# Head of a hybrid GLA / SSD layer: conditioning tiles issued without waits, x of block 0 normalised on ScalarE, five conditioning tiles contracted on TensorE, first weight units loaded and split first

## The reference, cut to what matters

```python
c_act = silu(c)
ada = c_act @ ada_w + ada_b                      # 1024 -> 3 x 1024
shift, scale, gate = split(ada, 3)
h = rms_norm(x, pre_norm_w) * (1 + scale) + shift    # x: 2048 x 1024
proj = h @ w_in
...
mixed = concat(gla(proj), ssd(proj)) @ w_out
x = x + gate * rms_norm(mixed, post_norm_w)
```

## Time and profile before

| | |
|---|---|
| median of 3 runs | 1800.64 us (1799.56 to 1802.90) |
| profiled execution | 1801.82 us |
| its span, first to last instruction | 1800.1 us |
| TensorE busy in the span | 1670.9 us (93%) |
| VectorE, ScalarE, POOL busy | 876.5, 784.0, 242.2 us |
| mean granted TensorE clock | 0.971 of full speed |

### The profile page before, as it was taken

How to read it: one execution, slowest core, us unless ns; L and a number is a source line. 1 busy time by engine, 2 the same in 40 slices (tenths; PEclk the granted TensorE clock), 3 DMA queues, 4 the chain that set the end, 5 groups by cost and what they waited for, 6 DMA issues and landing times. The chain is left out here.

```text
span 1800.1 us, 27177 instructions
## 1 busy us (share of the span) xinstructions
PE 1670.9 (93%) x10134; PEld 1431.9 (80%) x10134; DVE 876.5 (49%) x1603; ACT 784.0 (44%) x1390; POOL 242.2 (13%) x369
## 2 busy tenths in 40 slices
PE   3688899998999999989999999999999599999998
PEld 2477788887888888878888887888888377888886
DVE  5344344454434443355776668776777442222221
ACT  4354565444444554454455555455444431111110
POOL 5000000010000000000221222222222100000000
PEclk9799999999999999999999999999999799999999
DMA  9321242234222421224111234122110263222221
GB/s 278 130 89 60 82 148 86 66 117 141 77 65 64 142 65 59 82 59 135 65 66 64 93 102 138 65 72 92 66 52 35 103 235 117 93 93 93 93 99 41
DMA packets 105344, 172.23 MB, mean 96 GB/s; under 512 B 7587, under 2 KB 75443, under 8 KB 102310
## 3 DMA queue, kind: packets, MB, share of 16 engines
q1 hardware_dynamic: 102118, 154.05, 26.5%
q10 hardware_dynamic: 2304, 16.78, 2.5%
q0 software_dynamic: 832, 0.22, 0.3%
HBM read 137.21 MB, written 33.82 MB: 95 GB/s over the span
## 5 line engine op out<-in xcount | busy, mean ns | idle before, releaser
L1026 PE MATMUL ps<-hl,w 128*128 128x512 f32 x1488 | 377.5, 403 | 0.1
L1913 PE MATMUL ps<-d_w,d_yh 128*128 128x512 f32 x1536 | 353.0, 392 | 17.7 <-DVE d_yh L1870 11.0
L1913 PEld LDWEIGHTS ps<-d_w,d_yh 128*128 128x128 f32 x1536 | 289.5, 189 | 81.3 <-DVE d_yh L1870 11.4
L1026 PEld LDWEIGHTS ps<-hl,w 128*128 128x128 f32 x1488 | 276.9, 190 | 58.6 <-issue 1.4
L1646 PE MATMUL ps<-hl,w 128*128 128x256 f32 x2304 | 295.3, 288 | 4.3 <-PEq L258 4.3
L1646 PEld LDWEIGHTS ps<-hl,w 128*128 128x128 f32 x2304 | 283.2, 193 | 12.4 <-issue 12.4
L1032 PE MATMUL ps<-w,hl 128*128 128x256 f32 x1536 | 205.4, 291 | 2.0 <-DVE w L738 2.0
L1032 PEld LDWEIGHTS ps<-w,hl 128*128 128x128 f32 x1536 | 195.4, 195 | 4.9 <-DVE w L738 2.4
L1650 PE MATMUL ps<-hl 128*128 128x512 f32 x768 | 178.6, 391 | 0.0
L1528 DVE SCALAR_TENSOR_TENSOR c_acc<-c_before,conv_col,c_acc 128x256 f32<-128x256 f32 x288 | 142.1, 494 | 65.3 <-ACT c_acc L1412 58.3
L1650 PEld LDWEIGHTS ps<-hl 128*128 128x128 f32 x768 | 143.0, 188 | 29.2
(11 more groups left out here) (227 smaller groups left out, 2190.4 us busy)
## 6 DMA issues: line engine op xcount, KB each, us to landing
x_sb<-h SPq DMA_DIRECT2D x52, 512.0 KB, 3.9
c_ac<-step_sums ACTq DMA_DIRECT2D x16, 1024.0 KB, 4.7
w_raw<-in_w_in SPq DMA_DIRECT2D x30, 512.0 KB, 5.0
c_h_raw<-h SPq DMA_DIRECT2D x56, 256.0 KB, 2.8
d_y_raw<-mixed_in SPq DMA_DIRECT2D x7, 2048.0 KB, 9.1
ada<-in_ada_w SPq DMA_DIRECT2D x16, 512.0 KB, 11.4
x_sb<-in_x SPq DMA_DIRECT2D x16, 512.0 KB, 7.4
mixed_in<-y SPq DMA_DIRECT2D x32, 256.0 KB, 2.5
```

The costliest lines, as they stand in the source:

```text
L1026: mm = pe.matmul(ps[:, PROJ + u % 2, :], w[:, u, k, a, :], hl[:, par, k, b, :], start=(k == 0 and i == 0), stop=(k == KT - 1 and i == 2))
L1913: mm = pe.matmul(ps[:, 2 * t + j, :], yh[:, t, f, a, :], w[:, f, c, j * 512:(j + 1) * 512], start=(f == 0 and i == 0), stop=(f == FT - 1 a ...
```

## The change

The edits are all in `front`, in the part ahead of `step(0)`:

- SP: `load_ada` no longer waits. There are eight semaphores still, one for each pair of r in a half, and each reader waits for both tiles of a pair. x of block 0 is issued behind two conditioning tiles instead of one. w units 0 and 1 leave SP's stream. x of block 1 is issued ahead of w unit 2.
- ScalarE issues w units 0 and 1 as its first instructions, on its own queue. It normalises x of block 0, with four activations, in VectorE's place. `w_high` of units 0 and 1 stands ahead of the eight `first_copy`. `w_high` of unit 2 and the squares of block 1 stand behind the last `high`, ahead of `code_part`.
- VectorE adds up conditioning tiles r = 3 to 7 of half 0 and r = 2 to 7 of half 1 (OWN = (3, 2) is the number that it leaves out). `w_low` of units 0 and 1 stands ahead of `gains(0)`, pairs 0 and 2 stand ahead of the additions of half 1, and `w_low` of unit 2 and `x_normed(1)` ahead of `code_sum(0)`.
- TensorE contracts the tiles that are left out, `mods_row(j, r)`: eight products with a tile as weights and a column of c_act. Those of half 0 stand ahead of the transposes, those of half 1 behind the units of k = 1 and k = 2.

```diff
--- before.py
+++ after.py
@@ -123,6 +123,7 @@
     MODS = (7, 5)
     STEPS = GH * NB
     HK = KT // 2
+    OWN = (3, 2)
     SIZES_AT, GATE_AT = NB + 1, NB + 2
 
     W_SLOTS = tuple(2 * u + 3 for u in range(UV))
@@ -259,10 +260,9 @@
             @block.sync
             def _(sp):
                 def load_ada(j, r):
-                    wait(sp, ada_loaded[r], j * 16)
                     src = ada_w[0, r * P:(r + 1) * P, 0:2 * D].rearrange("p (s n) -> p s n", s=2)
                     sp.dma_start(ada[:, j, r, :].rearrange("p (s n) -> p s n", s=2), src[:, :, j * HK * P:(j + 1) * HK * P]
-                                 ).then_inc(ada_loaded[r], 16)
+                                 ).then_inc(ada_loaded[j * HK + r // 2], 16)
 
                 def load_x(b):
                     wait(sp, turned, b * KT)
@@ -313,14 +313,12 @@
                 sp.dma_start(c_col[:, :], c.rearrange("a (k p) -> p (a k)", p=P), allow_slow_non_contiguous=True).then_inc(c_loaded, 16)
                 for r in range(KT):
                     load_ada(0, r)
-                    if r == 0:
+                    if r == 1:
                         load_x(0)
-                load_w(0, 0)
-                load_w(0, 1)
                 for r in range(KT):
                     load_ada(1, r)
+                load_x(1)
                 load_w(0, 2)
-                load_x(1)
                 for k in range(KT):
                     store_h(0, k)
                 load_w(0, AHEAD)
@@ -632,6 +630,9 @@
                         if m >= NB and i in H_SLOTS:
                             again_high(m, H_SLOTS.index(i))
 
+                for u in range(2):
+                    src = column(0, u)
+                    act.dma_start(w_raw[:, u], w_rows[:, :, src:src + P]).then_inc(raw_loaded[u], 16)
                 act.wait_ge(c_loaded, 16)
                 act.activation(c_act[:, :], c_col[:, :], ACT.Silu).then_inc(c_ready, 1)
                 act.preload_act_table_set("natural_log_exp_and_others")
@@ -643,10 +644,13 @@
                 act.wait_ge(consts_ready, 10)
                 act.activation(w2[0:RANK, :], w2_raw[:, :], ACT.Copy).then_inc(w2_hi, 1)
                 act.activation(w2[R0:R0 + RANK, :], w2_raw[:, :], ACT.Copy).then_inc(w2_hi, 1)
+                act.wait_ge(xrstd_ready, 1)
+                for t in range(TB):
+                    act.activation(x_sb[:, t, :], x_sb[:, t, :], ACT.Copy, scale=x_rstd[:, t:t + 1]).then_inc(xn_ready, 1)
+                w_high(0, 0)
+                w_high(0, 1)
                 for k in range(KT):
                     first_copy(k)
-                w_high(0, 0)
-                w_high(0, 1)
                 for k in range(0, KT, 2):
                     act.wait_ge(gain_ready, k // HK + 1)
                     if k == 0:
@@ -654,15 +658,14 @@
                     even_full(0, k, first_full[:, k, :])
                     high(0, k)
                     high(0, k + 1)
-                    if k == HK - 2:
-                        w_high(0, 2)
+                w_high(0, 2)
+                for t in range(TB):
+                    x_square(1, t)
                 code_part(0)
                 evacuate(0, 0)
                 evacuate(0, 1)
                 code_high(0)
                 w_high(0, 3)
-                for t in range(TB):
-                    x_square(1, t)
                 for n in range(STEPS):
                     step(n)
 
@@ -888,12 +891,12 @@
                                       ALU.mult).then_inc(gate_step, 1)
 
                 def add_ada(j, r):
-                    dve.wait_ge(ada_loaded[r], (j + 1) * 16)
-                    if r == 0:
+                    dve.wait_ge(ada_loaded[j * HK + r // 2], 32)
+                    if r == OWN[j]:
                         dve.tensor_scalar(ada_sum[:, j, :], ada[:, j, r, :], c_act[:, r:r + 1], None, ALU.mult
                                           ).then_inc(sum_ready, 1)
                     else:
-                        dve.wait_ge(sum_ready, j * KT + r)
+                        dve.wait_ge(sum_ready, j * (KT - OWN[0]) + r - OWN[j])
                         dve.scalar_tensor_tensor(out=ada_sum[:, j, :], in0=ada[:, j, r, :], scalar=c_act[:, r:r + 1],
                                                  in1=ada_sum[:, j, :], op0=ALU.mult, op1=ALU.add).then_inc(sum_ready, 1)
 
@@ -912,35 +915,31 @@
                     low(0, k + 1)
 
                 dve.wait_ge(c_ready, 1)
-                for r in range(KT):
+                for r in range(OWN[0], KT):
                     add_ada(0, r)
-                    if r == KT // 2:
-                        x_normed(0)
                 dve.wait_ge(wg_hi, 1)
                 dve.tensor_tensor(wg[:, :, L0:L0 + RC], wg_raw[:, :, :], wg[:, :, 0:RC].bitcast(F32),
                                   ALU.subtract).then_inc(wg_ready, 1)
                 dve.wait_ge(w2_hi, 2)
                 dve.tensor_tensor(w2[L0:L0 + RANK, :], w2_raw[:, :], w2[0:RANK, :].bitcast(F32),
                                   ALU.subtract).then_inc(w2_ready, 1)
+                w_low(0, 0)
+                w_low(0, 1)
                 dve.wait_ge(cols_loaded, 32)
                 gains(0)
                 dve.wait_ge(first_raw, KT)
                 first_pair(0)
-                w_low(0, 0)
-                w_low(0, 1)
-                for r in range(KT):
+                first_pair(2)
+                for r in range(OWN[1], KT):
                     add_ada(1, r)
-                    if r == 1:
-                        first_pair(2)
-                    if r == 3:
-                        w_low(0, 2)
                 gains(1)
                 first_pair(4)
                 first_pair(6)
+                w_low(0, 2)
+                x_normed(1)
                 code_sum(0)
                 code_low(0)
                 w_low(0, 3)
-                x_normed(1)
                 for n in range(STEPS):
                     step(n)
 
@@ -974,10 +973,18 @@
 
             @block.tensor
             def _(pe):
-                def mods(j):
-                    pe.wait_ge(sum_ready, (j + 1) * KT)
+                def mods_row(j, r):
+                    pe.wait_ge(ada_loaded[j * HK + r // 2], 32)
+                    for f in range(KT):
+                        pe.matmul(ps[:, MODS[j], f:f + 1], ada[:, j, r, f * P:(f + 1) * P], c_act[:, r:r + 1], start=False,
+                                  stop=False)
+
+                def mods_start(j):
                     bias = ada_col[:, :].rearrange("p (s k) -> p s k", s=2)[:, :, j * HK:(j + 1) * HK]
                     pe.matmul(ps[:, MODS[j], 0:KT].rearrange("p (s k) -> p s k", s=2), ident[:, :], bias, start=True, stop=False)
+
+                def mods(j):
+                    pe.wait_ge(sum_ready, (j + 1) * KT - sum(OWN[:j + 1]))
                     for f in range(KT):
                         mm = pe.matmul(ps[:, MODS[j], f:f + 1], ada_sum[:, j, f * P:(f + 1) * P], ones[:, 0:1], start=False,
                                        stop=(f == KT - 1))
@@ -1131,14 +1138,22 @@
                             sum_gate()
 
                 pe.wait_ge(consts_ready, 8)
+                pe.wait_ge(c_ready, 1)
+                pe.wait_ge(cols_loaded, 32)
+                mods_start(0)
+                for r in range(OWN[0]):
+                    mods_row(0, r)
                 pe.wait_ge(xn_ready, TB)
                 for k in range(KT):
                     wait(pe, first_raw, k - 3)
                     turn_x(0, k, FIRST_TURNS[k % 4])
-                pe.wait_ge(cols_loaded, 32)
                 mods(0)
+                pe.wait_ge(first_raw, KT)
+                mods_start(1)
                 for k in range(HK):
                     first_units(k)
+                    if 0 < k <= OWN[1]:
+                        mods_row(1, k - 1)
                 mods(1)
                 for k in range(HK, KT):
                     first_units(k)
```

## The result

| | before | changed |
|---|---|---|
| median | 1800.39 us (6 runs, 1799.56 to 1802.90) | 1787.65 us (6 runs, 1784.45 to 1791.43) |
| ratio | | 0.9929, 95% interval 0.9916 to 0.9942 |
| profiled execution, span | 1801.82, 1800.1 us | 1787.65, 1785.9 us |
| first unit, second gains G, T | 36.65, 57.42, 82.36 | 37.25, 52.80, 69.97 |

The kernel is 12.7 us (0.7%) faster by medians and 14.2 by the spans of the two profiled executions. The forecast was 1791.0 in a range of 1786 to 1796.5, on the scale of the median.

What follows compares the result with a forecast made beforehand. TensorE's waits for x and VectorE were taken to bound the head. T comes 9.6 us earlier, 7.3 of it from G to T; 1801.82 less 9.6 gives 1792.2, on the median's scale 1791.0, range 1786 to 1796.5.

Steps and rivals of the forecast that it cites:

- first unit: Start of TensorE's first unit products in the head: forecast at 37.1 us, against 36.65 before.
- second gains G: Time when the gains of the second modulation are ready: forecast 55.2 us, 2.2 us earlier than before.
- T: First transpose of block 1 on TensorE: forecast 72.8 us, 9.6 us earlier; its shift carries to the end.
- Loads: DMA at the start: w adds 2.45 us ahead of x, ada tile 1 2.0; last x tile at 18.3 us.
- The first gains: Gains of the first modulation: forecast 34.4 us, set by VectorE and the loads, 2.2 us later than before.
- the clock charge ahead of G: TensorE before the second gains: one stretch of about 3.4 us at half speed, charged as 1.7 us.
- What bounds G: Before the second gains: VectorE's additions end under TensorE's work; two rows moved to TensorE cost 3.9 us and still pay.
- Behind T: After block 1's first transpose: no gain counted, at most 3.1 us more if the shorter wait keeps TensorE's clock high.
- Only the back half pays: Rival: second gains stay about 57.4 us, only the order behind them gains; 1792 to 1796.5 us, chance 0.26.
- Clock low throughout: Rival: TensorE slow at every step before the second gains, which come at 62.4; 1798 to 1802.5 us, chance 0.07.
- mutual slowing of the queues: Rival: three DMA queues slow each other from the start, tile 7 near 55 us, kernel about 1817 us; chance 0.05.
- The change does not do what it says: Rival: early w or fewer additions would bring nothing alone; no own chance, covered by the back-half case's time.

Runs made afterwards that it cites:

- the kernel with w on SP: Changed kernel with w units 0 and 1 loaded by SP again, behind the conditioning tiles of half 0, engine orders unchanged: 1795.49 us, ratio 0.9970.
- the kernel with the early split: Changed kernel with w_low of unit 0 moved ahead of conditioning tile 6 on VectorE: 1788.04 us, ratio 0.9929.
- the combined kernel: Changed kernel with one conditioning tile of half 1 on TensorE, code_sum ahead of block 1's normalising, and one w split earlier: 1783.84 us, ratio 0.9913.
- the kernel with the front half only: Changed kernel with the order behind the second gains put back as before the change: 1794.15 us, ratio 0.9957.
- the simple one: Changed kernel with no row of half 0 and one of half 1 on TensorE, code_sum ahead of block 1's normalising: 1783.09 us, ratio 0.9900.
- the two halves: Kernel before with only block 1's squares and normalising moved forward: 1791.89 us; changed kernel with the order behind the second gains put back: 1794.15 us.

## Why the prediction was right or wrong

**The mechanism and the sign were right, the size was short by a quarter.** At T 9.6 us were forecast and 12.4 came; by medians 12.7 against 9.6, between the two profiled executions 14.2. By steps:

- *Loads.* The last x tile was put at 18.3, it came at 18.56. That the sum came out was luck, for its two terms were off against each other: w adds 3.5 us, not 2.45, the conditioning tile 1.2, not 2.0 (the kernel with w on SP). w did not pass half ahead of x but wholly, and cost 3.5 us so, not the 4.9 of the upper bound. Packets did pass about one for one (774 and 746 from 8 to 18 us), but the count left out c, whose thousand small packets keep SP's queue busy while w goes ahead. Tiles 6 and 7 were put at 28.1, VectorE had them at 28.35.
- *x of block 0.* Normalised by 25.6, forecast 26.1. Right, with POOL's pow at 1.05 us instead of 2.0.
- *The first gains.* Forecast 34.4, copied at 34.51, behind the w splits as said. But the kernel with the early split shows that VectorE's hold was thin: in the executions where the clock rises late, TensorE's column ends within 1 us of VectorE's splits, and with one of the splits moved ahead it sets the gains itself. "VectorE and the loads set it" holds for the changed kernel's profiled execution, by 1.5 us (33.03 against 34.51), but not with the edit that was to make use of it.
- *First unit.* 37.1 forecast, 37.25 measured.
- **The step that failed is the clock charge ahead of G.** I charged 1.7 us for products with one column not holding the clock, a stretch of 3.4 us at half speed that no row of the kernel before shows. No such stretch came: from 43.30 to 52.40 the granted clock is 1.00. G was 52.80 against my 53.5 without the charge and 55.2 with it; the 0.7 left are units and columns that took a little less than their rows of before.
- *What bounds G.* "VectorE's additions under TensorE" was right (47.21 against 52.40). The sentence that the two rows "still pay" was wrong for one of them: with one row G and T are earlier, since VectorE has 3.3 us to spare with two. With no row of half 1 no kernel was run; an estimate from the combined kernel, where VectorE ended its seventh addition at 47.62 and the column began at 47.68, is that an eighth (1.36 us) would put G back by about 1.3 us, so that the one row probably pays. How the 2.9 us by which the column starts earlier divide between fewer additions and the splits of w that moved out of them was not separated.
- *G to T.* Forecast 17.6 with a wait of about 2 us for the gate product, measured 17.17 and 2.06.
- **Behind T** I counted nothing and named 3.1 us as the most. T to Z is 1709.4 us before and 1707.6 after. It lies close behind T: to the last group of units ahead of block 1's code (L1026 at 118.73, L1033 at 104.33) it is 36.4 us before and 34.4 after. The clock of that stretch rose from 0.80 to 0.93. That the shorter wait ahead of T is the cause does not fit the other kernels: the same stretch takes 34.4 us in the kernel with the front half only, where the wait is 8.97 us, and 35.8 in the combined and the simple one, where the waits are under 0.4. Over all kernels it takes 33.0 to 36.4 us with the same instructions; a group of twelve unit products in it takes 2.9 to 4.9 us, by where the rises and falls of the clock happened to lie. So the 1.8 us behind T, which are of two single executions, are not shown to be a gain of the change; by medians it is 12.7 us, and 12.4 of them are there at T.
- *Rivals.* "Only the back half pays" is refuted by the kernel with the front half only (1794.15). Clock low throughout and mutual slowing of the queues did not occur: up to 21.43 us the DMA engines moved 271 GB/s, against 261 before. "The change does not do what it says" holds of two of its parts: the three early rows, and the loads without waits (put back into the changed kernel, the waits cost nothing). It does not hold of w, which the new order needs early.

Of the 4.6 us between forecast and measurement on the profiled execution (1792.2 to 1787.65), 2.4 are at G (1.7 of them the clock charge), 0.4 between G and T, and 1.8 behind T.

## What to carry to other kernels

Look for work of the next block that stands behind finished work of this one in an in-order stream: moving four squares and four multiplications forward brought 8.8 us without saving an instruction. When work is shifted from an engine that is waited for to the one that waits, stop when both end together: here VectorE was done 3.3 us before TensorE's column began, and giving one row back to it took that row's 1.84 us off the path. What one part gains can be lost in a wait that another part makes, so the gains of the two halves, measured one by one (8.8 and 5.9 us at T), add to more than the gain of the whole (12.4).

## What the runs showed of the hardware

**The clock rose among transposes.** In the kernel before, TensorE had only idled until 24.96 us, and within its 32 transposes the time of one changed from 215 ns to 124. In all kernels that run the 32 in one stretch they took 5.12 to 6.61 us, depending on when the change came, and the column behind them ran at the high level (1.84 to 1.95 us). The granted clock reads 1.00 in all of the head up to the first fall, also where durations are those of the low level (3.57 us for the 16 pieces at 21.43 us, against 1.84 at 43.30), so ahead of the first fall the durations have to be read instead. The Trainium skill (TensorE: Matmul & The Clock Gate, Part 4: PE-mode transpose) says that transposes do not count as the engine being busy; here the trace disagrees.

**Among one-column products the clock stayed up, but did not rise.** Of the 9.1 us from 43.30 to 52.40, 5.5 were such products, and it stayed at 1.00; whether they held it or the units between them did was not separated. In the kernel before the same column at 53.47 us ran at the low level (3.55 us), behind 6 us of waiting. And the 32 pieces from 11.41 us on, 6.99 us without a gap, ran at the low level to their end (218 ns each, against 115 at 43.30), as did the 16 at 21.43 (223 ns), while transposes did see the clock rise.

**Small transfers beside large packets.** While POOL's column loads pass, now at 26 to 32 us, SP's queue is again slow; in the 8 us before them the core's DMA moved 383 to 389 GB/s. The DMA rows of the changed kernel in that stretch (packets, MB, share of 16 engines):

```profile
q1 hardware_dynamic: 327, 0.63, 94.6%
q0 software_dynamic: 261, 0.04, 42.1%
```

0.63 MB in 6 us are 105 GB/s. In the kernel before SP's packets there were w's of 512 B, 0.11 MB in the worst 2 us. Larger packets (2 KB now) did not clearly help. SP's queue in the changed kernel from 28 to 30 us, then in the kernel before from 26 to 28:

```profile
q1 hardware_dynamic: 87, 0.17, 92.8%
...
q1 hardware_dynamic: 328, 0.17, 70.4%
```

Both moved 0.17 MB in 2 us.
